# Latent attention: no-position queries and keys produced head by head with tokens along the free dimension, latent columns scaled before their transposes

## The reference, cut to what matters

```
h = rms_norm(x, attn_norm);  proj = h @ w_in          # 3648 columns
c_q, c_kv, k_rope, ... = split(proj)                  # 384, 128, 64 columns, ...
q  = (rms_norm(c_q, q_norm)  @ w_uq ).reshape(256, 8, 128 + 64)
kv = (rms_norm(c_kv, kv_norm) @ w_ukv).reshape(256, 8, 128 + 128)
q  = concat(q[..., :128], rope(q[..., 128:]))         # no-position part, rotated part
k  = concat(kv[..., :128], rope(k_rope) for every head);  v = kv[..., 128:]
out_a = softmax(chunk-causal mask of (q @ k^T) * 192^-0.5) @ v      # the latent attention
```

## Time and profile before

| | us |
|---|---|
| median of 3 runs | 2993.04 (2992.13 to 2995.12) |
| the profiled execution, its own time | 2994.43 |
| its span, first to last instruction | 2992.6 |
| PE busy | 2883.1 |
| PE weight load busy | 2432.3 |
| DVE busy | 1878.2 |
| ACT busy | 1478.6 |
| mean granted TensorE clock, share of full | 0.993 |

### The profile page before, as it was taken

How to read it: one execution, slowest core, us unless ns; L and a number is a source line. 1 busy time by engine, 2 the same in 40 slices (tenths; PEclk the granted TensorE clock), 3 DMA queues, 4 the chain that set the end, 5 groups by cost and what they waited for, 6 DMA issues and landing times.

```text
span 2992.6 us, 35219 instructions
## 1 busy us (share of the span) xinstructions
PE 2883.1 (96%) x13776; PEld 2432.3 (81%) x13776; DVE 1878.2 (63%) x2387; ACT 1478.6 (49%) x2038; POOL 46.5 (2%) x60
## 2 busy tenths in 40 slices
PE   5898998999999999999999999999999999999998
PEld 5786777888888888788888888888887888888887
DVE  7897998769855557555444554545566554445554
ACT  4436544565547654644334444455645443344443
POOL 0000000000000000000000000000000000000000
PEclk9999999999999999999999999999999999999999
DMA  9994687757655544555555555555455555555664
GB/s 385 329 348 171 221 313 300 270 181 252 228 175 168 171 140 154 170 185 187 190 194 193 183 185 195 178 181 162 141 160 170 188 184 191 195 189 184 202 192 141
DMA packets 173045, 609.66 MB, mean 204 GB/s; under 512 B 19360, under 2 KB 19632, under 8 KB 172240
## 3 DMA queue, kind: packets, MB, share of 16 engines
q1 hardware_dynamic: 170912, 600.42, 60.0%
q0 software_dynamic: 1824, 6.61, 0.8%
q10 hardware_dynamic: 144, 0.39, 0.0%
HBM read 605.24 MB, written 2.10 MB: 203 GB/s over the span
## 4 chain that ended last, share of the span: by engine, by line
PE 83%; DVE 8%; ACT 4%; DMA 3%; issue 2%; SPq 0%; POOL 0%; POOLq 0%; ACTq 0%; DVEq 0%
PE ps L1913 26%; PE ps L1916 25%; PE ps L1920 25%; DVE w_lo L1219 2%; PE ps L1872 2%; DVE raw L1327 2%; PE ps L2063 1%; PE ps L2047 1%; ACT w_hi L881 1%; PE ps L1930 1%; DMA raw<-in_w_modT 1%; ACT probs L1083 1%; DMA raw<-in_w_inb 0%; DMA raw<-in_w_in 0%; DMA raw<-in_w_ina 0%
## 5 line engine op out<-in xcount | busy, mean ns | idle before, releaser
L1219 DVE TENSOR_TENSOR w_lo<-raw,w_hi 128x1024 fp32r<-128x1024 f32 (+4 forms) x988 | 1157.9, 1176 | 968.3 <-ACT w_hi L881 964.1
L881 ACT ACTIVATE w_hi<-raw 128x1024 fp32r<-128x1024 f32 (+4 forms) x988 | 1003.1, 1019 | 1232.1 <-PE ps L1920 1058.8
L1913 PE MATMUL ps<-w_hi,hT_hi 128*128 128x512 f32 (+3 forms) x2848 | 762.7, 389 | 23.7 <-DVE proj L1304 13.4
L1916 PE MATMUL ps<-w_lo,hT_hi 128*128 128x512 f32 (+3 forms) x2848 | 737.1, 380 | 0.7 <-DVE w_lo L1219 0.7
L1920 PE MATMUL ps<-w_hi,hT_lo 128*128 128x512 f32 (+3 forms) x2848 | 733.8, 379 | 0.0
L1913 PEld LDWEIGHTS ps<-w_hi,hT_hi 128*128 128x128 f32 x2848 | 518.4, 189 | 114.1 <-DVE proj L1304 18.1
L1916 PEld LDWEIGHTS ps<-w_lo,hT_hi 128*128 128x128 f32 x2848 | 533.5, 189 | 90.8 <-DVE w_lo L1219 1.3
L1920 PEld LDWEIGHTS ps<-w_hi,hT_lo 128*128 128x128 f32 x2848 | 532.0, 188 | 88.4
L1913 PE MATMUL ps<-w_hi,uT_hi 128*128 128x512 f32 x1024 | 275.7, 390 | 0.0
L1920 PE MATMUL ps<-w_hi,uT_lo 128*128 128x512 f32 x1024 | 274.4, 389 | 0.0
L1916 PE MATMUL ps<-w_lo,uT_hi 128*128 128x512 f32 x1024 | 274.4, 389 | 0.0
(11 more groups left out here) (248 smaller groups left out, 1502.2 us busy)
## 6 DMA issues: line engine op xcount, KB each, us to landing
raw<-in_w_up SPq DMA_DIRECT2D x256, 512.0 KB, 3.5
raw<-in_w_down SPq DMA_DIRECT2D x256, 512.0 KB, 3.5
raw<-in_w_modT SPq DMA_DIRECT2D x192, 512.0 KB, 5.7
raw<-in_w_rest SPq DMA_DIRECT2D x80, 456.0 KB, 3.4
raw<-in_w_z SPq DMA_DIRECT2D x64, 512.0 KB, 4.8
raw<-in_w_out SPq DMA_DIRECT2D x64, 512.0 KB, 4.2
raw<-in_w_rest SPq DMA_DIRECT2D x48, 344.0 KB, 3.7
raw<-in_w_oa SPq DMA_DIRECT2D x32, 512.0 KB, 3.5
```

The lines of the kernel that those rows point to most:

```text
L881: act.activation(hi_blocks(L % SPLIT_SLOTS, c, w), blocks(raw, G % RAW_SLOTS, c, w), ACT.Copy).then_inc(S.hi_ready, 1)
L1219: dve.tensor_tensor(blocks(w_lo, r, c, w), blocks(raw, r, c, w), hi_blocks(s, c, w).bitcast(F32), ALU.subtract).then_inc(S.group_read, 1)
L1913: pe.matmul(o, rows(hi, c, t), wh[:, c], start=start and c == 0, stop=False)
L1916: pe.matmul(o, rows(hi, c, t), wl[:, c], start=False, stop=False)
```

## The change

Columns of the two weight matrices are reordered on the host, so that all heads' no-position columns come first. `uq` becomes `uqn` (1024 columns, 4 steps) and `uqr` (512, 2 steps), `ukv` becomes `ukn` (1024, 2 steps) and `uv` (1024, 2 steps). For `uqn` and `ukn` the weight block of a head is the stationary operand and 256 tokens are moving, so that the product lands as [128 columns of a head, 256 tokens], which is the layout of `qaT` and `kaT`; one ACT copy of 1024 columns takes a tile there. The eight prep entries for `qaT` and `kaT` go. DVE applies the norm's per-token factor to the latent columns ahead of their transposes, and PE's transposes of them wait for it. The slot weights of `mix_mla` are new, and `mla.roped` is 0.

```diff
-        yield f"uq{l}", "w_uq_2", l, 0, 3, 0, HA * (NOPE + ROPE), COLS
-        yield f"ukv{l}", "w_ukv_2", l, 0, 1, 0, HA * (NOPE + VA), COLS
+        yield f"uqn{l}", "w_uq_2", l, 0, 3, 0, HA * NOPE, COLS
+        yield f"uqr{l}", "w_uq_2", l, 0, 3, HA * NOPE, HA * ROPE, COLS
+        yield f"ukn{l}", "w_ukv_2", l, 0, 1, 0, HA * NOPE, COLS
+        yield f"uv{l}", "w_ukv_2", l, 0, 1, HA * NOPE, HA * VA, COLS
         yield f"rest2{l}", "w_in_2", l, 0, KC, 3 * tile, 5 * tile, tile
...
     v = w[k0 * P:(k0 + chunks) * P, col0:col0 + ncols].reshape(chunks, P, tiles, width)
     return np.concatenate([v[k:k + per].transpose(2, 1, 0, 3).reshape(tiles, -1) for k in range(0, chunks, per)], axis=1)
+
+
+def heads_apart(w, first):
+
+    v = w.reshape(*w.shape[:2], HA, -1)
+    return np.concatenate([part.reshape(*w.shape[:2], -1) for part in (v[..., :first], v[..., first:])], axis=2)
...
-        qm = A2("qm", [P, TOK, HA * (NOPE + ROPE)])
-        y_mla = qm[:, :, 0:HA * VA]
+        y_mla = A2("y_mla", [P, TOK, HA * VA])
+        qr = y_mla[:, :, 0:HA * ROPE]
         kv_at = A2.end
-        kv = A2("kv", [P, TOK, HA * (NOPE + VA)])
+        kv = A2("kv", [P, TOK, HA * VA])
...
-        rt = A2k("rt", [P, 2, COLS])
-        lam4 = A2k("lam4", [P, 4, HD])
-        lamt = A2k("lamt", [P, 2, HD])
-        A2q = Area(A2.end)
-        cT_hi = A2q("cT_hi", [P, 4, 2 * P], F32R)
-        cT_lo = A2q("cT_lo", [P, 4, 2 * P], F32R)
+        rt = at("rt", [P, 2, COLS], F32, A2.end)
+        cT_hi = A2("cT_hi", [P, 4, 2 * P], F32R)
+        cT_lo = A2("cT_lo", [P, 4, 2 * P], F32R)
         qaT = A2("qaT", [P, HA, 2 * P])
+        lam4 = A2("lam4", [P, 4, HD])
+        lamt = A2("lamt", [P, 2, HD])
...
                 product(f"c2{l}", hT), product(f"in2{l}", hT),
-                product(f"uq{l}", cT), product(f"ukv{l}", cT, lhs0=3), product(f"rest2{l}", hT),
+                product(f"uqn{l}", cT), product(f"uqr{l}", cT), product(f"ukn{l}", cT, lhs0=3),
+                product(f"uv{l}", cT, lhs0=3), product(f"rest2{l}", hT),
                 *[product(f"{name}{l}", hT, lhs0=k0, evac="dve") for name, k0 in (("oa", 0), ("ob", 8), ("oc", 12))],
...
             lead(f"out{l}", *after(f"out{l}", -5, -4, -3, -2, -1, 0, 3, 4))
-            lead(f"uq{l}", *after(f"uq{l}", -3, -2))
+            lead(f"uqn{l}", *after(f"uqn{l}", -3, -2))
...
         mla.scores = mla_scores
-        mla.v = lambda h, kk: kv[:, kk, h * 256 + NOPE:(h + 1) * 256]
-        mla.prep = (head_pairs(qm, 0, 192, NOPE, HA, qaT)
-                    + head_pairs(kv, 0, 256, NOPE, HA, kaT)
-                    + [([(0, P, flat(qrT[:, h:h + 2]))], [q_rope[:, t, 2 * (h + a):2 * (h + a) + 2].rearrange("p h d -> p (h d)")
+        mla.v = lambda h, kk: kv[:, kk, h * VA:(h + 1) * VA]
+        mla.prep = ([([(0, P, flat(qrT[:, h:h + 2]))], [q_rope[:, t, 2 * (h + a):2 * (h + a) + 2].rearrange("p h d -> p (h d)")
                                                           for a in range(2) for t in range(TOK)]) for h in range(0, HA // 2, 2)]
                     + [([(0, ROPE, krT[0:ROPE, 0]), (ROPE, P, krT[ROPE:P, 1])],
                         [k_rope[:, t].rearrange("p h d -> p (h d)") for t in range(TOK)])])
-        mla.roped = HA
+        mla.roped = 0
...
             return jobs["z0" if l == 0 else "rest1"].L + 2, jobs[f"z{l}"].L + 31, mix1_slots(l)
 
         def mix_mla(l):
-            return jobs[f"rest2{l}"].L + 2, jobs[f"rest2{l}"].L + 28, [1] * (1 + mla.slots(l))
+            return jobs[f"rest2{l}"].L + 2, jobs[f"rest2{l}"].L + 28, [0.3, 2] + [1] * (mla.slots(l) - 1)
...
                     return
+                if kind in ("uqn", "ukn"):
+                    b, dst = bank(job, i, 0), (qaT if kind == "uqn" else kaT)[:, 4 * i:4 * i + 4]
+                    act.activation(dst.rearrange("p h n -> p (h n)"), ps[:, b:b + 2].rearrange("p b n -> p (b n)"), ACT.Copy
+                                   ).then_inc(S.act_evacuated, 1)
+                    return
                 for t in range(TOK):
                     src = ps[:, bank(job, i, t), 0:job.width]
                     c = job.col0 + i * job.width
                     f, scale = ACT.Copy, 1.0
                     if kind == "z":
                         dst, f = proj[:, t, c:c + job.width], ACT.Silu
-                    elif kind == "uq":
-                        if i == 0 and t == 0:
-                            act.wait_ge(S.rstd_ready, rstd_value(l, 1))
-                        dst, scale = qm[:, t, c:c + job.width], stat[:, 12 + t:13 + t]
-                    elif kind == "ukv":
-                        dst, scale = kv[:, t, c:c + job.width], stat[:, 14 + t:15 + t]
+                    elif kind == "uqr":
+                        dst = qr[:, t]
+                    elif kind == "uv":
+                        dst = kv[:, t, i * COLS:(i + 1) * COLS]
...
 
-                dve.wait_ge(S.act_evacuated, jobs[f"ukv{l}"].E + 4)
+                dve.wait_ge(S.act_evacuated, jobs[f"uv{l}"].E + 2)
                 tmp = [rt[:, i // 2, (i % 2) * 2 * P:(i % 2 + 1) * 2 * P] for i in range(4)]
                 for t in range(TOK):
-                    q = qm[:, t].rearrange("p (h d) -> p h d", h=HA)
+                    q = qr[:, t].rearrange("p (h d) -> p h d", h=HA)
                     cos, sin = K["cos2"][:, 32 * t:32 * t + 32], K["sin2"][:, 32 * t:32 * t + 32]
-                    link(rotate(lambda a, b: q[:, :, NOPE + a:NOPE + b], repeat(cos, HA), repeat(sin, HA), 32,
+                    link(rotate(lambda a, b: q[:, :, a:b], repeat(cos, HA), repeat(sin, HA), 32,
...
                 variance([(4, 6, C_CKV), (6, 8, C_KR - C_CKV)])
+                walk.upto(c2.L + 19)
+                rstd()
+                for j, (t, c0, c1) in enumerate(((0, C_CQ2, C_CKV), (1, C_CQ2, C_CKV), (0, C_CKV, C_KR), (1, C_CKV, C_KR))):
+                    c = proj2[:, t, c0:c1]
+                    dve.tensor_scalar(c, c, stat[:, 12 + j:13 + j], None, ALU.mult).then_inc(S.c_scaled, 1)
                 first, last, slots = mix_mla(l)
...
                                before.E + T - 2 - before.T + 1)
+                if job.kind in ("uqn", "ukn"):
+                    heads_product(job, i, j, L, led_to).then_inc(S.group_multiplied, 1)
+                    return
...
+            def heads_product(job, i, j, L, led_to):
+
+                k0, cnt = job.groups[j]
+                start, stop = k0 == 0, k0 + cnt == job.chunks
+                terms = [(c, h, ps[:, bank(job, i, h // 2), h % 2 * 2 * P:(h % 2 + 1) * 2 * P])
+                         for c in range(cnt) for h in range(4)]
+                wh = hi_blocks(L % SPLIT_SLOTS, cnt, job.width)
+                wl = blocks(w_lo, group_at[L] % RAW_SLOTS, cnt, job.width)
+                at0 = job.lhs0 + k0
+                pe.wait_ge(S.hi_ready, L + 1)
+                if led_to:
+                    pe.wait_ge(S.lhs_hi, led_to[0])
+                for c, h, o in terms:
+                    pe.matmul(o, wh[:, c, h * P:(h + 1) * P], cT_hi[:, at0 + c],
+                              start=start and c == 0 and h % 2 == 0, stop=False)
+                pe.wait_ge(S.group_read, group_at[L] + 1)
+                for c, h, o in terms:
+                    pe.matmul(o, wl[:, c, h * P:(h + 1) * P], cT_hi[:, at0 + c], start=False, stop=False)
+                if led_to:
+                    pe.wait_ge(S.lhs_ready, led_to[1])
+                for c, h, o in terms:
+                    mm = pe.matmul(o, wh[:, c, h * P:(h + 1) * P], cT_lo[:, at0 + c], start=False,
+                                   stop=stop and c == cnt - 1 and h % 2 == 1)
+                return mm
+
             def lead_chunk(job, c, t):
 
...
                     pe.wait_ge(S.dve_evacuated, last.E + b // 2 + 1)
-                elif kind == "uq":
-                    pe.wait_ge(S.act_evacuated, jobs[f"c2{l}"].E + 2)
+                elif kind == "uqn":
+                    pe.wait_ge(S.c_scaled, 4 * (l + 1))
...
                 yield
-                pe.wait_ge(S.act_evacuated, jobs[f"ukv{l}"].E + 4)
+                pe.wait_ge(S.act_evacuated, jobs[f"uv{l}"].E + 2)
...
     a = {k: np.asarray(v) for k, v in inputs.items()}
```

More of the change, by code:

```diff
@@ L319, in build @@
         kaT2 = at("kaT2", [P, 4, 2, 2 * P], F32, A2.end)
-        A2k = Area(A2.end)
         kaT = A2("kaT", [P, HA, 2 * P])
-        rt = A2k("rt", [P, 2, COLS])
-        lam4 = A2k("lam4", [P, 4, HD])
-        lamt = A2k("lamt", [P, 2, HD])
-        A2q = Area(A2.end)
-        cT_hi = A2q("cT_hi", [P, 4, 2 * P], F32R)
-        cT_lo = A2q("cT_lo", [P, 4, 2 * P], F32R)
+        rt = at("rt", [P, 2, COLS], F32, A2.end)
+        cT_hi = A2("cT_hi", [P, 4, 2 * P], F32R)
+        cT_lo = A2("cT_lo", [P, 4, 2 * P], F32R)
         qaT = A2("qaT", [P, HA, 2 * P])
+        lam4 = A2("lam4", [P, 4, HD])
+        lamt = A2("lamt", [P, 2, HD])
         A2v = Area(kv_at)
@@ L342, in build @@
```

(8 more changed lines are left out.)

## The result

The median of 17 runs is 2999.20 us against 2992.13 us of the kernel before, run 17 times beside it: +7.1 us, ratio 1.0022 with a 95% interval of 1.0016 to 1.0029, so +4.8 to +8.7 us. The forecast was +7.4, 3000.4 us. In short: the removed transposes save some 3.3 us a layer, but PE now stands about 5 us a layer waiting for the rotation, and its clock is at half rate for a few microseconds around the end of that wait.

What follows compares the result with a forecast made beforehand. PE bounds the stage, except for ACT in its last four steps. Per layer +0.2 - 3.4 + 5.2 + 1.7 = +3.7, two layers +7.4, giving a median of 3000.4 us; range 2996.5 to 3007.5.

Steps and rivals of the forecast that it cites:

- The wait: Early in the latent attention, PE stands idle until DVE's rotation is signalled: 5.2 us a layer.
- The step that decided: PE meets the rotation wait ahead of rest2's step 2, at +5.07 us after step 0; the signal comes at +10.22.
- Rival 2: PE reaches the first transposes no earlier than the rotation is done: -3.2 us a layer, 2986.6 us; chance 0.09.
- The clock: PE's granted clock falls to 0.50 for a stretch after the stall: 1.7 us a layer, bounds nothing and 3.3.
- rival 1: PE stalls for the rotation but loses nothing to a low clock: 2.0 us a layer, 2997.0 us; chance 0.15.
- The transposes: Four slots of eight PE transposes each fall away in a layer of the latent attention: -3.4 us a layer.
- The latent products: Narrower matmuls in uqn and ukn, less shorter waits for ACT: +0.2 us a layer, bounds -0.6, +3.2 and +9.
- The distance at 256 columns: Matmuls with 256 moving columns in uqn and ukn start 0.120 us apart, read off a line through wider ones.
- rival 3: 256-column matmuls dearer, at 0.157 us: 6.7 us a layer, 3006.4 us; at 0.227 about 3018; chance 0.13.
- The evacuations: In uqn and ukn one ACT copy of 1024 columns replaces two of 512 taking 1.27 us, saving 0.2 us.
- The reading of the earlier trace: Eight 64-column matmuls with weight loads take 1.00 us, at most 0.125 each, so loads don't forbid 0.107.
- The scaling: DVE's four operations on the latent columns, at most 2.1 us, end before PE's transposes need them: cost nothing.

Runs made afterwards that it cites:

- run 17: Not a label of a run: the kernel before, unchanged, was run 17 times beside the changed kernel; its median is 2992.13 us.
- experiment 2: Changed kernel with PE's own shares 1.5 and 0.8 for slots 0 and 1, ACT and DVE weights 0.5 and 1.8 (rotation one split later): 2984.94 us.
- experiment 4: Changed kernel with 22 calls of identity matmuls ahead of PE's wait for the rotation, filling it: 2995.38 us, ratio 1.0009 to the kernel before.
- Experiment 5: Kernel before with only the wait for the rotation moved from prep entry 8 to entry 0: 3007.04 us, ratio 1.0049.
- experiment 1: Changed kernel with PE's own shares 1.5 and 0.8 for slots 0 and 1, so three steps pass ahead of its wait: 2984.66 us, ratio 0.9977.
- experiment 7: Changed kernel with shared slot weights 0.5 and 1.8 for all engines, none of PE's own: 2998.37 us, ratio 1.0023 to the kernel before.
- experiment 6: Kernel before with only the latents' scaling on DVE and uq and ukv evacuated without a factor: 2990.97 us, ratio 1.0000.
- experiment 8: The kernel of experiment 2 with each head-wise matmul cut in two of 128 moving columns: 3001.96 us, ratio 1.0029 to the kernel before.
- experiment 3: Changed kernel with 45 calls of identity matmuls ahead of PE's wait for the rotation, outlasting it: 3003.95 us, ratio 1.0042 to the kernel before.

## Why the prediction came out

**The wait.** The step that decided held to 0.1 us: PE's slot 1 stands ahead of step 2, and the signal comes 10.12 us after step 0, for 10.22. The wait's part is 5.03 us in layer 0 and 5.06 in layer 1 (experiments 2 and 4) for 5.2. Experiment 5 makes the same loss in the kernel before out of one number, experiment 1 takes it out of the changed one by PE's order alone. Rival 2, the wait is met, is what experiments 1 and 2 build: they gain 6.8 and 6.5 us over the kernel before, where the rival's price was 6.4.

**The clock.** 1.84 us in layer 0 and 1.67 in layer 1 for 1.7. It falls in both layers, so rival 1 did not happen; with the wait filled (experiment 4) the kernel is rival 1, +2.7 us by the ratio for +4.0. Its length was not settled by the rows of before. In layer 1 it was as forecast, 3.4 us at 0.50 with PE at work throughout. In layer 0 it lasted 6.8 us, the first 2.9 of them in the wait itself and 3.9 of them at work, so that the loss came near 1.7 by luck; in experiments 5 and 7 it lasted 6.8 us too, and cost more, some 2.7 and 2.4. In the traces the five low stretches of 6.8 us all began while PE still stood, 1.2 to 3.0 us before it went on, and the one of 3.4 us began 0.2 us after it was at work again. Whether that decides between the two lengths stays open, with a single case on one side. The two low stretches of the changed kernel:

```profile
984.85:991.68 6.83, 3.88 (x14) 3.66 (x15) 4.75 (x14) 0.00 (x0) 0.00 (x0) 0.50 0.08 34
...
2032.74:2036.15 3.41, 3.41 (x14) 3.17 (x13) 1.70 (x2) 0.00 (x0) 0.00 (x0) 0.50 0.00 0
```

**The transposes.** -3.32 us a layer for -3.4.

**The latent products.** The term that was off. Forecast +0.2, measured -0.35 in layer 0 and -0.39 in layer 1. The distance at 256 columns was right, 0.120, and rival 3 fell with it. The evacuations were mis-sized: I let the 1024-column copies save 0.2 us and the others nothing, and all of them lost 0.2. Evacuation without a factor gives -0.68 by itself (experiment 6), the head-wise products then cost 19.10 - 18.77 = +0.33. The reading of the earlier trace rows as a sign that the loads leave room down to 0.107 us was loose: a record there (of plain float32) lasts 0.27 us, so the eight are on average (1.00 - 0.27) / 7 = 0.104 apart with 64 columns, where the columns alone are 0.027. So the row held a floor a little under 0.120, and experiment 8 then measured one of 0.112 for fp32r.

**The sum.** -0.35 - 3.32 + 5.03 + 1.84 = +3.20 in layer 0, against +3.7; in layer 1, -0.39 - 3.39 + 5.06 + 1.67 = +2.95. The two layers give +6.15, the medians +7.1 with an interval that holds both. So the terms add up to 1.3 us less than the forecast of +7.4, nearly all of it the latent products' term, and that the medians lie within 0.3 us of the forecast is chance.

**The scaling** costs nothing, as forecast. The bound of 2.1 us for its four operations didn't follow from 0.69 each, which is 2.8; measured they took 1.14, so nothing hung on it.

## What to carry to other kernels

In a schedule that several engines walk through by one list of shares, look at what each engine does with an empty share: here one engine did a slot behind its share and another ahead of it, and the share that was to hold back a wait put the work behind it. Before moving a wait forward, set down both times from one common point, that of the waiting engine and that of the signal; the difference was right to 0.2 us, and it was larger than all that the change saved. Where stretches between fixed points repeat to half a microsecond and whole runs scatter by several, compare the stretches.

## What the runs showed of the hardware

A plain float32 matmul on the identity leaves two records, each 0.112 us behind the last at 2.4 GHz (45 calls gave 90 in experiment 3, 22 gave 44 in experiment 4), while a transpose leaves one (two entries of four give eight in the earlier trace rows). The products with the values are plain float32 calls as well, and in the kernel before the latent attention's 48 calls left 96 records, so "eight matmuls" in the earlier trace rows are four calls. An fp32r matmul keeps its line of 0.417 ns a column plus 0.014 us down to 256 moving columns, with another weight block each time, and leaves it at 128, where it takes 0.112 us (experiment 8). ACT copies 512 columns out of PSUM in about 0.55 us without a per-partition factor and 0.64 with one (half of 1.09 and of 1.27). An idle wait of 4.5 to 5.0 us, as the profile gives it, was overlapped or followed by a granted clock of 0.50 in all three kernels that had it (the changed one, experiments 5 and 7) and in both layers, for 3.4 or 6.8 us.
